# A fused encoder layer: the opening reordered, and the gate logits made from split factors in earlier tiles

## The reference, cut to what matters

```
h = rmsnorm(x, attn_norm)                       # 1024 x 1024
z = h @ w_in                                    # columns: q, k, v, gate(16), g, cq(256), ckv(128), kpe(32)
gate_logit = zgate @ w_gate_up + b_gate         # (1024 x 16) @ (16 x 256)
log_a = max(log_sigmoid(gate_logit) / 16, -1)   # decays of the gated linear attention
o_gla = chunked gated linear attention(q, k, v, log_a), normalized, times silu(g)
o_mla = latent attention(rmsnorm(cq) @ w_uq, rmsnorm(ckv) @ w_ukv, kpe), block-causal
x = x + [o_gla, o_mla] @ w_out
x = x + relu(rmsnorm(x, mlp_norm) @ w_up)^2 @ w_down
```

## Time and profile before

| | us |
|---|---|
| median of 3 runs | 1139.67 |
| lowest and highest run | 1139.0, 1140.64 |
| the profiled execution, its own time | 1138.34 |
| its span, first to last instruction | 1136.3 |

### The profile page before, as it was taken

One profiled execution on the slowest core, in us unless ns is written; L12 is line 12 of the kernel. 1 busy time (PEld: TensorE's weight loads), 2 busy tenths in 40 slices (PEclk: granted clock), 3 DMA queues, 4 the chain that ended last, 5 costly groups with the idle time before them and its releaser, 6 DMA issues.

```text
span 1136.3 us, 15331 instructions
## 1 busy us (share of the span) xinstructions
PE 1117.2 (98%) x5616; PEld 904.0 (80%) x5616; DVE 776.2 (68%) x1125; ACT 465.1 (41%) x880; POOL 511.9 (45%) x418
## 2 busy tenths in 40 slices
PE   8999999999999999999999999999999999999998
PEld 6978888776676778887888888888878888888887
DVE  4566766657777752178485875586696888888863
ACT  5353544335555552156223323332434334434341
POOL 2332513214443462238654445444635656555562
PEclk9999999999999999999999999999999999999999
DMA  7242523361221116213443333330789793456642
GB/s 252 69 130 74 167 81 115 106 205 33 61 65 48 34 38 241 74 75 112 152 144 135 125 112 130 131 129 35 253 276 362 246 288 121 140 184 222 206 118 85
DMA packets 98555, 158.41 MB, mean 139 GB/s; under 512 B 9329, under 2 KB 39041, under 8 KB 98482
## 3 DMA queue, kind: packets, MB, share of 16 engines
q1 hardware_dynamic: 96864, 152.80, 40.8%
q10 hardware_dynamic: 1298, 4.46, 1.2%
q0 software_dynamic: 320, 0.19, 0.2%
HBM read 115.47 MB, written 41.94 MB: 139 GB/s over the span
## 4 chain that ended last, share of the span: by engine, by line
PE 85%; DVE 8%; ACT 2%; issue 2%; POOL 1%; DMA 1%; ACTq 0%; SPq 0%; DVEq 0%
PE ps L1956 80%; PE ps L2224 2%; PE ps L2072 1%; DVE t_all L1728 1%; DVE dr_lo L1728 1%; DVE m_nm L1667 1%; POOL tx_lo L950 1%; PE ps L1971 1%; DVE xn L1372 1%; DMA gain<-in_attn_norm_dram 1%; DMA m_ukv<-in_w_ukv_dram 0%; ACT m_p L1193 0%; DVE state L1372 0%; DVE stage L1728 0%; DVE m_pT L1678 0%
## 5 line engine op out<-in xcount | busy, mean ns | idle before, releaser
L1956 PE MATMUL ps<-dr_hi,dl_hi 128*128 128x512 f32 x448 | 174.5, 390 | 1.6 <-DVE dr_lo L1728 1.6
L1956 PE MATMUL ps<-dr_hi,dl_lo 128*128 128x512 f32 x448 | 174.3, 389 | 0.0
L1956 PE MATMUL ps<-dr_lo,dl_hi 128*128 128x512 f32 x448 | 174.3, 389 | 0.0
L955 POOL TENSOR_TENSOR ua_lo<-up_raw,ua_hi 128x1024 fp32r<-128x1024 f32 x46 | 116.6, 2539 | 116.7 <-ACT ua_hi L993 116.7
L979 POOL TENSOR_TENSOR dl_lo<-l_raw,dl_hi 128x512 fp32r<-128x512 f32 x64 | 101.1, 1603 | 70.6 <-ACT dl_hi L993 70.2
L979 POOL TENSOR_TENSOR dl_lo<-s_all,dl_hi 128x512 fp32r<-128x512 f32 x48 | 74.4, 1569 | 59.0 <-ACT dl_hi L993 58.1
L1956 PEld LDWEIGHTS ps<-dr_hi,dl_hi 128*128 128x128 f32 x448 | 84.1, 188 | 20.3 <-issue 2.8
L1956 PE MATMUL ps<-a_hi,ua_hi 128*128 128x512 f32 x256 | 99.9, 390 | 0.0
L1956 PE MATMUL ps<-a_lo,ua_hi 128*128 128x512 f32 x256 | 99.6, 389 | 0.0
L1956 PE MATMUL ps<-a_hi,ua_lo 128*128 128x512 f32 x256 | 99.6, 389 | 0.0
L1956 PEld LDWEIGHTS ps<-dr_lo,dl_hi 128*128 128x128 f32 x448 | 84.1, 188 | 17.4
(11 more groups left out here) (250 smaller groups left out, 2536.3 us busy)
## 6 DMA issues: line engine op xcount, KB each, us to landing
r_raw<-in_w_down_dram SPq DMA_DIRECT2D x144, 256.0 KB, 3.4
hidden<-stage SPq DMA_DIRECT2D x72, 256.0 KB, 2.1
up_raw<-in_w_up_dram SPq DMA_DIRECT2D x16, 1024.0 KB, 5.4
l_raw<-hidden SPq DMA_DIRECT2D x64, 256.0 KB, 3.4
raw<-in_w_in_dram SPq DMA_DIRECT2D x24, 256.0 KB, 3.0
z_gla<-z_stage SPq DMA_DIRECT2D x16, 256.0 KB, 2.0
raw<-in_w_out_dram SPq DMA_DIRECT2D x16, 256.0 KB, 7.3
xs<-in_x_dram SPq DMA_DIRECT2D x8, 512.0 KB, 9.3
```

Source lines behind the costliest of these rows:

```text
L955: pool.tensor_tensor(ua_lo[n % UP_RING][:, :, :], up_source(g, product), ua_hi[n % UP_RING][:, :, :].bitcast(F32), ALU.subtract).then_inc( ...
L1956: return pe.matmul(dst, lhsT, rhs, start=start, stop=stop, skip_group_check=onto)
```

## The change: what it does

The opening. `gain` is asked for by ScalarE's queue directly after x of block 1, with a semaphore of its own (`gain_all`). ScalarE then makes a one-column copy of the identity into PSUM, which brings its table load ahead; it squares x of block 0 and asks for x of block 2 before its copies. The copies of `xT0` change places: VectorE takes k = 0 to 3, ScalarE k = 4 to 7; the square of block 1 follows them, ahead of the first high part of the weights. TensorE makes three more transposes of the identity after those of `gain_row`.

The gate. ScalarE splits off `wgate_hi` and writes `zgateT_hi`; VectorE subtracts to get `wgate_lo` and the two halves of `zgateT_lo`, in its `behind(8)` ahead of `c_lo`. Each of the four logits is a split product. They stand at tile 9, k = 6; tile 10, k = 3; tile 11, k = 2 and k = 5, the last one in bank 7. The tile after each waits for VectorE's pass over it, the heads of block 1 for all four.

```diff
-FIRST_PRODUCTS = 10
+FIRST_PRODUCTS = 10, 3
...
-        zgateT = at("zgateT", [GR, T], 124 * KB)
+        zgateT_hi = at("zgateT_hi", [GR, T], 124 * KB, F32R)
+        zgateT_lo = at("zgateT_lo", [GR, T], 160 * KB, F32R)
...
-        LOGIT_TILES = (NB + 3, NB + 5, 2 * NB + 1, 2 * NB + 3)
+        LOGITS = (NB + 1, KT - 2, (NB + 2) % 3), (NB + 2, 3, (NB + 3) % 3), (NB + 3, 2, (NB + 4) % 3), (NB + 3, 5, 7)
...
                 if s == GATE_T:
+                    act.wait_ge(phase_in, 96)
+                    copy(wgate_hi[:, :], wgate[:, :])
                     act.wait_ge(gateT_ready, 1)
                     for i in range(2):
-                        copy(zgateT[:, i * W:(i + 1) * W], ps[0:GR, 5 + i, :]).then_inc(gateT_out, 1)
+                        copy(zgateT_hi[:, i * W:(i + 1) * W], ps[0:GR, 5 + i, :]).then_inc(gateT_out, 1)
...
             x_load(1)
+            act.dma_start(gain[:, :], attn_norm[0].partition_broadcast(P)).then_inc(gain_all, 16)
+
+            act.wait_ge(const_ready, IDENT)
+            step(copy(ps[:, 7, 0:1], ident[:, 0:1]))
+            x_square(0)
+            x_load(2)
 
             act.wait_ge(x0T_out2, 1)
-            act.wait_ge(xT_ready, 2)
-            for k in range(4):
-                copy(xT0[:, k, :], bank4(4)[:, k, :], gT[:, k:k + 1]).then_inc(x0T_out, 1)
-            act.dma_start(gain[:, :], attn_norm[0].partition_broadcast(P)).then_inc(gain_in, 16)
-            x_square(0)
-            in_high_part(0, 0)
-            x_load(2)
+            act.wait_ge(xT_ready, 3)
+            for k in range(4, KT):
+                copy(xT0[:, k, :], bank4(5)[:, k - 4, :], gT[:, k:k + 1]).then_inc(x0T_out, 1)
             x_square(1)
-            for k in range(1, 5):
+            for k in range(5):
                 in_high_part(0, k)
...
+                if s == GATE_T:
+                    dve.wait_ge(gateT_out, 2)
+                    dve.tensor_tensor(wgate_lo[:, :], wgate[:, :], wgate_hi[:, :].bitcast(F32), ALU.subtract)
+                    for i in range(2):
+                        half = slice(i * W, (i + 1) * W)
+                        dve.tensor_tensor(zgateT_lo[:, half], ps[0:GR, 5 + i, :], zgateT_hi[:, half].bitcast(F32),
+                                          ALU.subtract).then_inc(gateT_out, 1)
...
-            dve.wait_ge(xT_ready, 3)
-            for k in range(4, KT):
-                dve.tensor_scalar(xT0[:, k, :], bank4(5)[:, k - 4, :], gT[:, k:k + 1], None, ALU.mult).then_inc(x0T_out2, 1)
+            dve.wait_ge(xT_ready, 2)
+            for k in range(4):
+                dve.tensor_scalar(xT0[:, k, :], bank4(4)[:, k, :], gT[:, k:k + 1], None, ALU.mult).then_inc(x0T_out2, 1)
             first_low_part(0)
-            dve.wait_ge(gain_in, 32)
+            dve.wait_ge(gain_all, 16)
...
+                for n in range(FIRST_PRODUCTS[1]):
+                    pe.transpose(ps[:, 0, 0:P], ident[:, :], ident[:, :])
...
+            def logit(n):
+                s, _, bank = LOGITS[n]
+                t, i = logit_half(n)
+                pe.wait_ge(gateT_out, 4)
+                if bank == 7:
+                    pe.wait_ge(qkv_out, 1)
+                else:
+                    pe.wait_ge(z_out, s - 1)
+                dims, half = slice(t * P, (t + 1) * P), slice(i * W, (i + 1) * W)
+                split_product(ps[:, bank, :], wgate_hi[:, dims], wgate_lo[:, dims], zgateT_hi[:, half], zgateT_lo[:, half],
+                              True, True).then_inc(logit_ready, 1)
...
                     elif b == 1:
-                        pe.wait_ge(qkv_out, 1)
+                        pe.wait_ge(logit_out, 2 * GT)
```

More of the change, by code:

```diff
@@ L160, in layer @@
         wgate = at("wgate", [GR, GH * GDK], GB + 1280)
+        wgate_lo = at("wgate_lo", [GR, GH * GDK], GB + 1280, F32R)
+        wgate_hi = at("wgate_hi", [GR, GH * GDK], GB + 2304, F32R)
         zv = at("zv", [P, 2, W], 160 * KB)
@@ L278, in layer @@
         raw_in = [sem(f"raw_in{s}") for s in range(RING)]
-        x0T_out, x0T_out2 = sem("x0T_out"), sem("x0T_out2")
+        x0T_out, x0T_out2, gain_all = sem("x0T_out"), sem("x0T_out2"), sem("gain_all")
         gain_in, consts_in, phase_in, mla_w_in = sem("gain_in"), sem("consts_in"), sem("phase_in"), sem("mla_w_in")
@@ L1510, in behind @@
                     rotary_tables()
[L1511 to L1516, removed]
+                for n in range(len(LOGITS)):
+                    if s + 1 == LOGITS[n][0]:
+                        t, i = logit_half(n)
+                        dve.wait_ge(logit_ready, n + 1)
+                        dve.tensor_scalar(g_cum[:, t, i * W:(i + 1) * W], ps[:, LOGITS[n][2], :], bg[:, t:t + 1], LEAST_LOGIT,
+                                          ALU.add, ALU.max).then_inc(logit_out, 1)
                 b = prep(s, HEAD_NORMS)
@@ L1796, in _ @@
                 residual(0, b)
-            dve.wait_ge(gain_in, 48)
+            dve.wait_ge(gain_in, 32)
             def norm_two(pos):
@@ L1986, in first_tile @@
                     if k == KT - 2:
+                        pe.wait_ge(x0T_out, 4)
                         norm_T(1)
                     if k < 4:
-                        pe.wait_ge(x0T_out, k + 1)
+                        pe.wait_ge(x0T_out2, k + 2)
                     else:
-                        pe.wait_ge(x0T_out2, k - 2)
+                        pe.wait_ge(x0T_out, k - 3)
                     pe.wait_ge(*raw_landed(0, k))
@@ L1994, in first_tile @@
                 last.then_inc(z_ready, 1)
-            def logit(s):
-                n = LOGIT_TILES.index(s)
-                t, i = n // 2, n % 2
-                pe.wait_ge(phase_in, 96)
-                pe.wait_ge(z_out, s - 1)
-                mm(ps[:, (s + 1) % 3, :], wgate[:, t * P:(t + 1) * P], zgateT[:, i * W:(i + 1) * W],
-                   True, True).then_inc(logit_ready, 1)
+            def logit(n):
+                s, _, bank = LOGITS[n]
+                t, i = logit_half(n)
+                pe.wait_ge(gateT_out, 4)
[6 more added lines that the diff above has]
+                              True, True).then_inc(logit_ready, 1)
             def in_project(q, b, between=None):
@@ L2010, in in_project @@
                     pe.wait_ge(z_out, n - 2)
-                if n - 1 in LOGIT_TILES:
-                    pe.wait_ge(logit_out, LOGIT_TILES.index(n - 1) + 1)
+                if any(s == n - 1 for s, _, _ in LOGITS):
+                    pe.wait_ge(logit_out, sum(s < n for s, _, _ in LOGITS))
                 for k in range(KT):
@@ L2015, in in_project @@
                         between()
-                    if n in LOGIT_TILES and k == 3:
-                        logit(n)
+                    for i in range(len(LOGITS)):
+                        if LOGITS[i][0:2] == (n, k):
+                            logit(i)
                     if q == 0 and k % 4 == 0:
@@ L2088, in behind @@
                         pe.wait_ge(mla_lo, 1)
-                        pe.wait_ge(gateT_out, 2)
+                        pe.wait_ge(gateT_out, 4)
                     elif b == 1:
-                        pe.wait_ge(qkv_out, 1)
+                        pe.wait_ge(logit_out, 2 * GT)
                     else:
@@ L2115, in _ @@
             pe.wait_ge(const_ready, IDENT)
-            for n in range(FIRST_PRODUCTS):
+            for n in range(FIRST_PRODUCTS[0]):
                 pe.transpose(ps[:, 3, 0:P], ident[:, :], ident[:, :])
```

2 lines of the change are left out of this document (added).

## The result

The change made the kernel slower: 1141.94 us median (1138.78 to 1144.82, 19 runs) against 1139.18 (1137.59 to 1141.58, 19 runs), ratio 1.0024 [1.0016, 1.0031], some 2.8 us. The forecast was 1139.0 in a range of 1136.7 to 1141.2: wrong in sign and outside the range.

The account below looks back on a forecast made before the run. TensorE, busy 98% of the span, was taken as the bound. Opening -1.3 plus gate and logits +0.65 (-1.80 + 2.35 + 0.1) gave -0.65 us, put on the median as 1139.0, range 1136.7 to 1141.2.

Parts of the forecast that it names:

- So TensorE stands from 70.16 to 72.8, 2.65 us: Tile 9, k = 6: TensorE waits for the split gate ahead of the first new logit; +2.35 net, bounds 2.05 and 3.1.
- the 0.31 given back: Block 0's heads: their old 0.31 us wait for `c_lo` disappears, hidden behind the first logit's wait.
- a rival, but only in the opening: Opening: TensorE's clock rises late, low until tile 1 is through; +4.75, 1144.4 us, chance 0.10.
- Against it: Late-clock rival: loads idle 1.4 us before block 1's transposes at 15.40, yet those eight took 0.86, at the upper level.
- That fewer rows (16) are used gives nothing: I keep the row's slot: New logits: three products of 512 columns at 0.23 each, 0.69 per logit, despite only 16 rows.
- the term of -1.80: Four logit products: 4.56 us in the old form against 2.76 in the new, -1.80.
- The opening, -1.3: Up to tile 1: its first product starts near 16.15 and not 17.47; bounds 0 and 2.9.
- The last weight piece: Opening, SyncE's queue: the narrow 8 KB piece lands near 15.4 and limits when tile 1 starts.
- The estimate by turns: Opening, queues alternating by packet: ScalarE's transfers over near 10.2, last piece near 14.7, opening gives 2.0, sum 1138.3.
- The heads of block 1, +0.1 (0 to 0.6): Block 1's heads wait for all four logits: TensorE's 7.15 us against VectorE's 7.1, a tie taken as +0.1.
- What the opening gives up is not all handed on: From 26.5 to 55 us TensorE is always busy, so it hands on the opening's gain one for one.
- the tie: Block 1's heads: TensorE's 7.15 us against VectorE's 7.1; +0.1, bounds 0 and 0.6.

Follow-up runs that it names:

- gate_only: The kernel before with only the change's gate and logits, old opening kept: 1142.44 us (5 runs), ratio 1.0033.
- fill_wait: The changed kernel plus twenty transposes of the identity ahead of the first logit's wait: 1140.17 us (11 runs), ratio 1.0011.
- wide_logits: early_split with two of the four logits made from 128-row factors in place of the gate's 16 rows: 1138.07 us, a single run.
- begin_only: The kernel before with only the change's opening, old gate and logits kept: 1139.2 us (11 runs), ratio 1.0002.
- early_split: The changed kernel with the gate's transposes in tile 8 ahead of k = 3 and its splits ahead of `m_uq_hi` and `m_uq_lo`: 1137.86 us, ratio 0.9988.
- early_old_opening: early_split with the opening of the kernel before: 1137.31 us (11 runs), ratio 0.9984.
- early_x2_late: early_split with x of block 2 asked for behind the copies of `xT0` and the square of block 1: 1135.99 us (5 runs), ratio 0.9969.
- x2_late_pair: early_x2_late with the third and fourth logits as a pair at tile 11, k = 5: 1135.39 us (5 runs), ratio 0.9968.
- begin_x2_late: begin_only with x of block 2 asked for behind the square of block 1: 1138.61 us (11 runs), ratio 0.9997.
- gain_late: early_x2_late with `gain` also asked for behind ScalarE's copies: 1138.24 us (11 runs), ratio 0.9992.
- early_pairs: early_split with the logits two and two, at tile 10, k = 6 and tile 11, k = 5: 1137.83 us (11 runs), ratio 0.9986.

## Why the prediction was wrong, point by point

**The step that failed first: "So TensorE stands from 70.16 to 72.8, 2.65 us", priced as its length and nothing more.** The wait itself was right to 0.02 us (2.63), as were the two engines' order, the hidden `c_lo` and the 0.31 given back. The 0.02 is in part luck: `zgateT_hi` was ready 0.16 sooner after TensorE's arrival than forecast, and `wgate_lo`, put at 0.32, took 0.56. What was missing is what an idle TensorE costs afterwards: 3.4 us at 1.2 GHz, +1.5 in the trace of after, and twice that in gate_only's. fill_wait takes it away without shortening the wait, and the printed clock of the runs shows that it is the rule and not this one trace: 1 of 19 at 1.000 after, 7 of 11 with the fill; with the old opening, none of five in gate_only where before has 52 of 75.

**How it came to be missed.** I had the mechanism as a rival, but only in the opening, where I read it off the weight loads. Its "Against it" was that 1.4 us of idle loads before 15.40 had not lowered the clock. But only the loads had been idle so long. The products had stopped for 0.72 us (order of time on PE, before):

```profile
15.40 1.10 PE L1971 MATMUL ps<-ident,x 128*128 128x128 f32 x8 [0.72 <-DVE x L1372]
```

From one execution that was weak evidence even for its own length, as the 1.36 and 0.28 us before 850 in wide_logits show, and I never asked the question of the 2.65 us that I had just computed. The Trainium skill, TensorE: Matmul & The Clock Gate, section "HAM oscillation — how this bites in real kernels", describes this for waits longer than the one here: the stage behind such a wait begins at the low level, and what that costs is half of the time spent there. The trace agrees in the fall and nearly in its price, 1.5 of 3.4 us. It differs in that 2.6 us of wait were enough, and in that the low level began 1.7 us after the wait had ended (72.19 to 73.9). I had cited another section of the page and not weighed this one.

**"That fewer rows (16) are used gives nothing: I keep the row's slot", the term of -1.80.** Mis-sized. A logit costs 0.98 with 16 rows and 0.69 with 128 (wide_logits), so the term is 4 x (0.98 - 1.14) = -0.64. The row that I used, had no change of rows in it, while the other, the old logit's 1.14, did. The weight loads are not it: a load of 16 rows took 0.18 us and one of 128 rows 0.19. The Trainium skill, TensorE: Matmul & The Clock Gate, section "LDWEIGHTS (loading the stationary operand)", says that rows don't enter a load's time; by that rule, the trace agrees, and the 0.29 lies in the distances between products, 0.32, 0.34, 0.23 and 0.32 where neighbours have 0.23.

**The opening, -1.3.** Two landings were as forecast: `gain` at 9.42 ("by 10") and x of block 2 at 12.17 ("by 12.5"). The last weight piece landed at 14.67, sooner than "near 15.4". The estimate by turns had put it at 14.7, but had both of ScalarE's transfers over near 10.2. Tile 1 started at 16.61 ("near 16.2"), and the path to it was another than forecast: not the last piece held it, but the small piece of the third weight tile, asked for at 3.74 and landed at 11.37. From 11.51 on TensorE's products run without a gap up to tile 1, 1.9 us behind the last landing. And this is one execution. In five others with the change's own opening tile 1 starts at 16.37, 18.29, 17.92, 17.81 and 18.55; with after itself that is 17.59 in the mean, against 17.83 for the old opening in three (17.47, 18.30, 17.73). That is -0.24, and begin_only's ratio of 1.0002 and the pair early_split and early_old_opening agree with next to nothing. The reason is in the rows: while `gain` and x of block 2 pass, the weights starve, TensorE waits 0.8 twice or 2.03 once, and the clock rises with the weight loads' fall from 0.33 to 0.19 us anywhere between 8.6 and 14.2. The sum treated the opening as a matter of the last piece alone; the step that failed is that path. The Trainium skill, TensorE: Matmul & The Clock Gate, section "What's actually happening", says that this point moves from run to run. The traces agree that it moves, but over 5.6 us among kernels with this opening, which is far more than that section gives.

**The heads of block 1, +0.1 (0 to 0.6):** 0, within the bounds. **What the opening gives up is not all handed on:** The earlier trace rows showed TensorE without a gap up to 55 us, and I took that as far as tile 9; in tile 8 0.24 of the 0.86 goes back into a wait for `wi_lo`.

**The range.** Its upper end held the opening at 0, the wait at 3.1 and the tie at 0.6, and nothing for the clock. With -0.24, +2.32, +1.5 and -0.64 the sum is +2.9; the medians differ by 2.8. (The +0.26 is left out, since it is there only when tile 1 starts early.) That is closer than the terms deserve: of before's runs 23 in 75 have lost 1.7 already, 0.5 in the mean, and seven of the 19 after were low for longer than one stretch.

**Open.** Of the 3.2 us of early_x2_late the logits account for 0.64 and, in its one trace, the earlier tile 1 (16.02 against 17.47) for 1.45; the rest isn't explained. Also open: why early_x2_late and x2_late_pair have all their ten runs at 1.000 and begin_x2_late, with the same opening, six of 11; whether filling the opening's holes pays; and which executions fall twice. The fall's chance after a wait of a given length is known here only by counts.

## What to carry to other kernels

Price a wait on a TensorE that is otherwise full as its length plus the work that it then does at half clock, here 1.5 us for one of 2.5; if the wait can't be removed, useless matmuls in it gave half of the loss back. Before moving work earlier, look for the time at which its producers' engines idle: the same splits cost 4.1 us behind `m_ukv_lo` and nothing ahead of `m_uq_lo`. Look at the printed clock of every run and not at the profiled one alone, since a stall whose price is drawn by lot shows in the spread before it shows in a trace.

## What the runs showed of the hardware that I had not expected

- With a wait of 2.4 to 2.6 us in it, TensorE was granted 1.2 GHz, while busy, from 0.3 us before the wait's end (gain_late) to 1.7 behind it (after), for 3.4 us (after, gain_late) or 6.8 (gate_only). 18 of 19 runs of after and 5 of 5 of gate_only print a mean clock below 1.000. After 1.36 and 0.28 us it fell in one trace (wide_logits) and not in another (before); after 1.70 it fell (early_pairs), after 1.37 it didn't (gate_only's opening).
- In 3.4 us at 1.2 GHz 1.5 us were lost: products of 512 columns went from 0.23 to 0.43 us apart, of 384 columns from 0.18 to 0.32.
- With twenty transposes in the place of the idle time 7 of 11 runs print 1.000.
- A split product over 16 rows between such of 128 costs 0.98 us, over 128 rows 0.69; two over 16 rows in a row 1.68. The product behind it adds 0.12 in the 16-row cases.
- With both queues full from 6 to 9 us, ScalarE's moved 0.55 MB in 154 packets and SyncE's 0.37 MB in 454; the shares of engine time are 53.0% and 43.5%. One packet for one would have given equal counts, if both had work all the time, which this view can't show.
